# Two neighbouring rows of the down weights on one partition, and a strided transpose to match, in a streaming encoder step

## Chip, cores and metric

The kernel runs on one core of one Trainium2 chip. The metric is the device time of one execution in microseconds (us); the median of 3 runs is 1451.0 us, between 1450.89 and 1451.71.

## What is computed

One inference step of a two-layer encoder for 384 frames of width 1024 (256 of a new stream, 16 of each of 8 running ones). Each layer has a mixer (a causal convolution group and a pooling group between the projections w_in and w_out) and then a channel mixer: dense SwiGLU in layer 0, the two best of eight SwiGLU experts in layer 1. The channel mixers are what this case is about:

```python
D_MODEL, D_FF, EXPERT_FF, N_EXPERTS, TOP_K = 1024, 2816, 2816, 8, 2

def swiglu(h, wg, wu, wd):
    return jnp.einsum('blf,fd->bld',
                      jax.nn.silu(jnp.einsum('bld,df->blf', h, wg)) * jnp.einsum('bld,df->blf', h, wu), wd)

def moe_swiglu(h, router_w, router_b, wg, wu, wd):
    ...
    for e in range(N_EXPERTS):
        out = out + gates[..., e:e + 1].astype(h.dtype) * swiglu(h, wg[e], wu[e], wd[e])
    return out
```

All data are float32.

## The kernel before

Every engine's program is written out by hand, with semaphores between the engines; no scheduler moves anything.

**Precision.** A float32 product is made of three products of halves: a weight tile `raw` is copied to `w_hi` in a rounded form (ScalarE, `make_hi`, line 260), `w_lo = raw - w_hi` is made by VectorE (`make_lo`, line 264), and `product` (lines 284 to 286) issues three matmuls, hi by hi, hi by lo, lo by hi.

**Weight tiles.** The 2816 hidden columns of a channel mixer are cut into `NF` = 11 pieces of 256. A piece has three tiles of 1 MB (128 partitions of 2048 floats): gate and up (1024 input rows by 256 columns, in memory 1 KB runs), and down (256 hidden rows by 1024 columns, rows of 4 KB). `raw`, `w_hi` and `w_lo` have six slots each: two pieces. SyncE issues the loads in the order in which they are used (`sp_tile`, line 350, calls `load`, line 252): a slot's next load waits until `make_lo` has read the slot (`lo_ready`). ScalarE's `make_hi` waits for the landing, and, in `act_ffn_tile` (line 525), for the matmuls that read the slot of `w_hi` before.

**One unit**, that is one piece of 256 hidden columns for one block of 128 tokens. The dense mixer has 11 pieces for 3 blocks of tokens, 33 units; the expert mixer has one gathered block an expert, 8 x 11 = 88 units. 121 in all. On TensorE (`pe_unit`, line 1140) unit l makes

- `unit_gu` (line 1098): 24 matmuls of 512 columns, gate and up side by side into one PSUM bank, tokens on the partitions,
- `unit_turn` (line 1117) of the unit before: two transposes of `act_b` (128 tokens by 256 hidden columns), so that hidden rows lie on the partitions,
- `unit_down` (line 1123) of the unit two before: 12 matmuls of 512 columns with `ft_hi` and `ft_lo` (the transposed activations, halved by `act_ft`, line 538, and `ft_low`, line 835) as the loaded operand and the down tile as the streamed one.

In a transpose and in a matmul alike the first operand after the output is loaded into the array (LDWEIGHTS, the engine PEld of the profile) and the second streams through it. In `unit_turn` the loaded one is `act_b`, the streamed one the identity:

```python
for i in range(2):
    ins = pe.transpose(ps[:, f.bank(l), i * P:(i + 1) * P], act_b[:, i * P:(i + 1) * P], ident[:, :])
```

Transpose i gives hidden rows 128 i to 128 i + 127, so row p of half i on partition p; the source of a down tile (`ffn_src`, line 328) puts rows p and p + 128 on partition p, one after the other, which is what `unit_down` streams for i = 0 and i = 1.

Between experts TensorE gathers the next expert's tokens (`gather`, line 1167, 48 small matmuls) and scatters the last one's results (`scatter`, line 1178).

Of the kernel before, what the change touches and what calls it, by code (L numbers as in the profile page):

```python
# [25 lines left out]
P = 128  # L26
# [12 lines left out]
FT = 256  # L39
# [50 lines left out]
def build(nc, a):  # L90
    ctx = ExitStack()
    with ctx:
# [3 lines left out]
        def place(name, floats, dt=F32, offset=None, parts=P):  # L96
            o = at["next"] if offset is None else offset
            t = nc.alloc_sbuf_tensor_at(name, [parts, floats], dt, offset=base + o)
            if offset is None:
                at["next"] = (o + floats * 4 + 31) // 32 * 32  # L100
            at[name] = o
            return t
# [14 lines left out]
        ident = place("ident", P)  # L117
# [25 lines left out]
        act_b = place("act_b", FT, offset=s0 + 5120)  # L143
# [29 lines left out]
        ps = ctx.enter_context(nc.psum_tensor("ps", [P, 8, 512], F32))  # L173
# [17 lines left out]
        def y_sb(c):  # L191
            return ext[:, c * WIN:(c + 1) * WIN]

        def y_sq(c):
            o = NCB * CEXT + c * WIN
            return ext[:, o:o + WIN]
# [85 lines left out]
        def product(pe, out, lh, ll, rh, rl, start, stop):  # L282

            pe.matmul(out, lh, rh, start=start, stop=False)  # L284
            pe.matmul(out, lh, rl, start=False, stop=False)  # L285
            return pe.matmul(out, ll, rh, start=False, stop=stop)  # L286
# [41 lines left out]
        def ffn_src(w, kind, e, c):  # L328

            m = w[kind][0]  # L330
            if len(m.shape) == 3:
                if kind == "d":
                    rows = m.rearrange("e (c k p) n -> (e c) p k n", p=P, k=2)
                    return rows[bass.ds(e * NF + c, 1)].rearrange("o p k n -> (o p) k n")
                m = m[bass.ds(e, 1)].rearrange("o a b -> (o a) b")
            if kind == "d":
                return m[bass.ds(c * FT, FT), :].rearrange("(k p) n -> p k n", p=P)
            return m.rearrange("(k p) n -> p k n", p=P)[:, :, bass.ds(c * FT, FT)]


# [9 lines left out]
        def sp_tile(sp, f, w, e, kind, c, c_expr):  # L350
            load(sp, f.slot(kind, c), f.uses(kind, c), ffn_src(w, kind, e, c_expr), 2 if kind == "d" else KD)
# [730 lines left out]
        def _(pe):  # L1082
# [10 lines left out]
            def blk(ap, i, width=TOK):  # L1093
                return ap[:, i * width:(i + 1) * width]
# [22 lines left out]
            def unit_turn(f, l):  # L1117
                pe.wait_ge(S["act_done"], f.count(l + 1))
                for i in range(2):
                    ins = pe.transpose(ps[:, f.bank(l), i * P:(i + 1) * P], act_b[:, i * P:(i + 1) * P], ident[:, :])  # L1120
                ins.then_inc(S["turned"], 1)

            def unit_down(f, l, shift):
# [16 lines left out]
            def pe_unit(f, l, shift, item):  # L1140
                static = isinstance(f.step, int)
                true = l + shift if item is not None and static else None
                prev = item is not None and item.prev is not None
                if true == 0:
                    pe.wait_ge(S["xT_lo"], 2 * item.n + 2)
                unit_gu(f, l)
                if true == 0:
                    turn_one_hot(item)
                if prev and true in SCATTER:
                    scatter(item.prev[0], 1 - item.parity, SCATTER[true])  # L1150
                if l > 0 or prev:
                    unit_turn(f, l - 1)
                if l > 1 or prev:
                    if true == 2 and prev:
                        pe.wait_ge(S["ye_lo_ready"], 2 * item.prev[0] + 2)
                    unit_down(f, l - 2, shift)
                if true == 9 and item.nxt is not None:
                    gather(item.nxt[0])
# [30 lines left out]
            for l in range(LAYERS):  # L1189
                pe_hT(2 * l, range(NTB))  # L1190
                if l == 0:
# [5 lines left out]
                    for i in range(LAYERS):  # L1197
                        n = TAPS * NCB
                        ins = pe.transpose(ps[:, 6, C_CW + i * n:C_CW + (i + 1) * n],
                                           prm_rows[0:n, (1 + i) * P:(2 + i) * P], ident[0:n, 0:n])  # L1200
# [8 lines left out]
                for j in range(12):  # L1209
                    s, m = divmod(j, 2)  # L1210
# [9 lines left out]
                    for k in range(KD):  # L1220
                        o = s * TILE + k * 256 + m * P
                        ins = product(pe, ps[:, WIN_BANK[j], 0:TOK], w_hi[:, o:o + P], w_lo[:, o:o + P],
                                      blk(a_hi, k), blk(a_lo, k), k == 0, k == KD - 1)
                    ins.then_inc(S["blk_done"], 1)
                    if j == 1:
# [6 lines left out]
                        for c in range(NCB):  # L1232
                            for g in range(3):
                                rows = hist[0:120, g * CH + c * P:g * CH + (c + 1) * P]
                                ins = pe.transpose(ps[:, 2 + c, g * 120:(g + 1) * 120], rows, ident[0:120, 0:120])
# [38 lines left out]
                def w_out(s, tb):  # L1274
                    for i in range(2):
                        e = 2 * WOUT_TILES[s] + i
                        for dh in range(2):
                            o, m = e * TOK + tb * P, WOUT_SLOT[s] * TILE + i * D + dh * 512
                            ins = product(pe, ps[:, 2 * tb + dh, :], a_hi[:, o:o + P], a_lo[:, o:o + P],
                                          w_hi[:, m:m + 512], w_lo[:, m:m + 512], s == 0 and i == 0, s == 3 and i == 1)  # L1280
                    return ins
# [4 lines left out]
                for c in range(NCB):  # L1286
                    pe.wait_ge(S["y_ready"], 4 * l + c + 1)
                    ins = pe.matmul(ps[:, 6, 0:TOK], mean_w[:, :], y_sb(c), start=c == 0, stop=c == NCB - 1)  # L1288
# [3 lines left out]
                for tb in range(NTB):  # L1292
                    ins = w_out(0, tb)
                ins.then_inc(S["wout_used"], 1)
                pe.wait_ge(S["sq_done"], 4 * (l + 1))
                for c in range(NCB):
                    ins = pe.matmul(ps[:, 7, 0:TOK], mean_w[:, :], y_sq(c), start=c == 0, stop=c == NCB - 1)
                ins.then_inc(S["var_done"], 1)
                pe.wait_ge(lo_ready[WOUT_SLOT[1]], GEN_WOUT[l][1] + 1)
                for tb in range(NTB):  # L1300
                    ins = w_out(1, tb)
# [12 lines left out]
                if l == 0:  # L1314
                    pe_hT(1, [1])

                    def dense_unit(f, l, shift):
                        if l < NTB and shift == 0 and isinstance(f.step, int):
                            if l == 1:
                                pe_hT(1, [2])  # L1320
                            if l == 2:
                                pe.wait_ge(S["x_added"], 6)
                            pe.wait_ge(S["hT_lo"], ht_count(1, l, 1))
                        pe_unit(f, l, shift, None)
                    units_loop(pe, dense, dense_unit)
                    unit_turn(dense, DENSE_UNITS - 1)
                    unit_down(dense, DENSE_UNITS - 2, 0)
                    unit_down(dense, DENSE_UNITS - 1, 0)
# [5 lines left out]
            for k in range(KD):  # L1334
                ins = product(pe, ps[0:NE, 2, 0:TOK], rw_hi[:, k * NE:(k + 1) * NE], rw_lo[:, k * NE:(k + 1) * NE],
                              blk(a_hi, k), blk(a_lo, k), k == 0, k == KD - 1)
            ins.then_inc(S["logits_done"], 1)
            pe.wait_ge(S["lgt_ready"], 1)
            for tb in range(NTB):
                ins = pe.transpose(ps[:, 4, tb * NE:(tb + 1) * NE], lgt[0:NE, tb * P:(tb + 1) * P], ident[0:NE, 0:NE])  # L1340
# [6 lines left out]
            for tb in range(NTB):  # L1347
                ins = pe.matmul(ps[:, 3, (tb + 1) * NE:(NTB + 1) * NE], mean_w[:, :], mask[:, 0:(NTB - tb) * NE],
                                start=False, stop=tb == NTB - 1)
# [6 lines left out]
            def finish(f, item):  # L1356
                unit_turn(f, NF - 1)
                unit_down(f, NF - 2, 0)
                unit_down(f, NF - 1, 0)
                pe.wait_ge(S["ye_lo_ready"], 2 * item.n + 2)  # L1360
                scatter(item.n, item.parity, range(6))
# [145 lines left out]
```

## Time and profile before

| | |
|---|---|
| median of 3 runs | 1451.0 us |
| profiled execution, span from first to last instruction (no other time of this execution is listed) | 1453.4 us |
| TensorE matmul busy (PE) | 1380.2 us, 95% |
| weight loads into the array (PEld) | 1152.1 us, 79% |
| VectorE (DVE) | 1041.2 us, 72% |
| ScalarE (ACT) | 792.8 us, 55% |
| moved by DMA | 343.13 MB, mean 236 GB/s |

The span of the profiled execution is 2.4 us above the median. The dense mixer runs from about 165 us to 440 us of the span, the expert mixer from about 620 us to 1440 us. A matmul's end is modelled in the profile, so where matmuls follow each other the distance between two starts says what one costs, not its duration. "Landing" of a DMA is counted from its issue.

### The profile page before, as it was taken

To read this page: it belongs to the slowest core of one execution; us is meant where nothing else is said; L and a number is where in the kernel's file an instruction comes from. 1 tells how busy PE (TensorE), PEld (TensorE's weight loads), DVE (VectorE), ACT (ScalarE), POOL (GpSimd) and SP (SyncE) were. 2 spreads that over 40 slices of the span, in tenths; PEclk is the share of its full clock that TensorE was granted. 3 is DMA by queue.
4 is the path that set the end of the run, shared out by engine and by line. 5 is a ranking of instruction groups with operands and counts; after the bars stand their busy time and mean duration, and the time that the engine had idled before them with its cause. 6 is when DMAs were issued, how large, how long until landed. Compare 5 with 4: busy or idle time off the path is not lost.

```text
span 1453.4 us, 17788 instructions
## 1 busy us (share of the span) xinstructions
PE 1380.2 (95%) x6492; PEld 1152.1 (79%) x6493; DVE 1041.2 (72%) x1196; ACT 792.8 (55%) x892; POOL 69.2 (5%) x120
## 2 busy tenths in 40 slices
PE   5999899999998989689999999999999999999994
PEld 5986788888887977578888888888888888888883
DVE  4795633333327795568799798898887997997984
ACT  5554322232215553367677677665776766766752
POOL 1050100000000231000000000000000000000000
PEclk9999999999998999799999999999999999999997
DMA  9114433433143114379999999999999999999971
GB/s 314 67 53 159 159 116 119 141 117 117 51 150 98 47 52 124 111 261 366 332 344 358 326 348 363 312 342 367 328 347 321 348 353 324 354 355 323 346 261 70
DMA packets 252825, 343.13 MB, mean 236 GB/s; under 512 B 6252, under 2 KB 222724, under 8 KB 252758
## 3 DMA queue, kind: packets, MB, share of 16 engines
q1 hardware_dynamic: 249542, 335.78, 68.6%
q0 software_dynamic: 1424, 4.31, 1.0%
q10 hardware_dynamic: 1792, 2.18, 0.4%
q8 instruction: 39, 0.64, 0.2%
q14 instruction: 28, 0.23, 0.0%
HBM read 339.01 MB, written 3.23 MB: 235 GB/s over the span
## 4 chain that ended last, share of the span: by engine, by line
PE 85%; DVE 10%; ACT 2%; issue 1%; DMA 1%; POOL 0%; SPq 0%; DVEq 0%; POOLq 0%; ACTq 0%
PE ps L284 26%; PE ps L286 25%; PE ps L285 25%; DVE ps L818 5%; PE ps L1173 3%; PE ps L1120 2%; DVE w_lo L264 1%; DMA raw<-in_w_in 1%; PE ps L1184 1%; PE ps L1186 1%; PE ps L1288 1%; DVE ext L778 1%; ACT ext L504 1%; DVE x L900 1%; DVE a_lo L785 1%
## 5 line engine op out<-in xcount | busy, mean ns | idle before, releaser
L264 DVE TENSOR_TENSOR w_lo<-raw,w_hi 128x2048 fp32r<-128x2048 f32 x317 | 717.2, 2288 | 126.9 <-ACT w_hi L260 126.7
L260 ACT ACTIVATE w_hi<-raw 128x2048 fp32r<-128x2048 f32 x317 | 596.3, 1916 | 4.9 <-DMA raw<-in_w_in 4.1
L284 PE MATMUL ps<-w_hi,a_hi 128*128 128x512 f32 x1064 | 419.8, 395 | 8.2 <-DVE ft_lo L838 5.5
L286 PE MATMUL ps<-w_hi,a_lo 128*128 128x512 f32 x1064 | 415.7, 391 | 0.0
L285 PE MATMUL ps<-w_lo,a_hi 128*128 128x512 f32 x1064 | 415.7, 391 | 0.0
L543 ACT ACTIVATE ft_hi<-ps 128x256 fp32r<-128x256 f32 x121 | 46.5, 385 | 390.5 <-PE ps L1120 390.5
L284 PEld LDWEIGHTS ps<-w_hi,a_hi 128*128 128x128 f32 x1064 | 200.6, 189 | 54.3 <-issue 8.4
L286 PEld LDWEIGHTS ps<-w_hi,a_lo 128*128 128x128 f32 x1064 | 200.5, 188 | 42.0
L285 PEld LDWEIGHTS ps<-w_lo,a_hi 128*128 128x128 f32 x1064 | 200.7, 189 | 41.3 <-issue 0.6
L284 PE MATMUL ps<-w_hi,ft_hi 128*128 128x512 f32 x484 | 200.9, 415 | 0.0
L286 PE MATMUL ps<-w_hi,ft_lo 128*128 128x512 f32 x484 | 191.5, 396 | 0.0
L285 PE MATMUL ps<-w_lo,ft_hi 128*128 128x512 f32 x484 | 191.1, 395 | 0.0
L838 DVE TENSOR_TENSOR ft_lo<-ps,ft_hi 128x256 fp32r<-128x256 f32 x121 | 51.0, 421 | 146.7 <-ACT ft_hi L543 146.7
L818 DVE SCALAR_TENSOR_TENSOR ps<-ext,prm,ps 128x256 f32<-128x256 f32 (+1 forms) x360 | 109.9, 397 | 0.0
L286 PEld LDWEIGHTS ps<-w_hi,ft_lo 128*128 128x128 f32 x484 | 91.3, 189 | 20.7
L285 PEld LDWEIGHTS ps<-w_lo,ft_hi 128*128 128x128 f32 x484 | 91.9, 190 | 16.4
L284 PEld LDWEIGHTS ps<-w_hi,ft_hi 128*128 128x128 f32 x484 | 92.1, 190 | 16.0
L284 PE MATMUL ps<-a_hi,w_hi 128*128 128x384 f32 x192 | 66.3, 345 | 6.6 <-DVE a_lo L785 6.6
L1377 POOL TENSOR_TENSOR stat<-stat,mhalf 128x1 f32<-128x1 f32 x15 | 12.2, 817 | 1187.0 <-DVE stat L771 1187.0
L285 PE MATMUL ps<-a_lo,w_hi 128*128 128x384 f32 x192 | 65.4, 341 | 0.0
L286 PE MATMUL ps<-a_hi,w_lo 128*128 128x384 f32 x192 | 65.3, 340 | 0.0
L832 DVE TENSOR_TENSOR act_b<-ps,silu 128x256 f32<-128x256 f32 x121 | 50.5, 417 | 8.8 <-ACT silu L536 8.8
(151 smaller groups left out, 957.7 us busy)
## 6 DMA issues: line engine op xcount, KB each, us to landing
raw<-in_moe_w_gate SPq DMA_DIRECT2D x88, 1024.0 KB, 7.5
raw<-in_moe_w_up SPq DMA_DIRECT2D x88, 1024.0 KB, 8.3
raw<-in_moe_w_down SPq DMA_DIRECT2D x88, 1024.0 KB, 7.5
raw<-in_w_in SPq DMA_DIRECT2D x12, 1024.0 KB, 12.0
raw<-in_dense_w_gate SPq DMA_DIRECT2D x11, 1024.0 KB, 5.4
raw<-in_dense_w_up SPq DMA_DIRECT2D x11, 1024.0 KB, 5.4
raw<-in_dense_w_down SPq DMA_DIRECT2D x11, 1024.0 KB, 5.0
raw<-in_w_out SPq DMA_DIRECT2D x8, 1024.0 KB, 5.1
```

Of the source, the lines that this page charges most:

```text
L260: act.activation(slot(w_hi, s), slot(raw, s), ACT.Copy).then_inc(hi_ready[s], 1)
L264: dve.tensor_tensor(slot(w_lo, s), slot(raw, s), slot(w_hi, s).bitcast(F32), ALU.subtract)\
L284: pe.matmul(out, lh, rh, start=start, stop=False)
L285: pe.matmul(out, lh, rl, start=False, stop=False)
L286: return pe.matmul(out, ll, rh, start=False, stop=stop)
L504: act.activation(ext[:, tb * D:(tb + 1) * D], x[:, tb * D:(tb + 1) * D], ACT.Square, accum_out=stat[:, tb:tb + 1]).then_inc(S["ssq_done"], 1)
L543: act.activation(ft_hi[:, b * FT:(b + 1) * FT], ps[:, f.bank(l), 0:FT], ACT.Copy)\
L818: ins = dve.scalar_tensor_tensor(out=o, in0=src, scalar=w, in1=o, op0=ALU.mult, op1=ALU.add)
L832: dve.tensor_tensor(act_b[:, :], ps[:, f.bank(l), FT:2 * FT], silu[:, :], ALU.mult)\
L838: dve.tensor_tensor(ft_lo[:, b * FT:(b + 1) * FT], ps[:, f.bank(l), 0:FT], ft_hi[:, b * FT:(b + 1) * FT].bitcast(F32), ALU.subtract)\
L1120: ins = pe.transpose(ps[:, f.bank(l), i * P:(i + 1) * P], act_b[:, i * P:(i + 1) * P], ident[:, :])
L1173: ins = pe.matmul(ps[:, 2 + i, (k % 4) * P:(k % 4 + 1) * P], h[:, tb * D + k * P:tb * D + (k + 1) * P], onehot[:, tb * P:(tb + 1) * P], st ...
```

## The change

The down tile's source has rows 2p and 2p + 1 of the 256 on partition p, which lie next to each other in memory: 8 KB in one run where there were two runs of 4 KB. The two transposes take the even and the odd columns of `act_b`, so that half i of the transposed activations has hidden row 2p + i on partition p.

```diff
                 if kind == "d":
-                    rows = m.rearrange("e (c k p) n -> (e c) p k n", p=P, k=2)
+                    rows = m.rearrange("e (c p k) n -> (e c) p k n", p=P, k=2)
                     return rows[bass.ds(e * NF + c, 1)].rearrange("o p k n -> (o p) k n")
                 m = m[bass.ds(e, 1)].rearrange("o a b -> (o a) b")
             if kind == "d":
-                return m[bass.ds(c * FT, FT), :].rearrange("(k p) n -> p k n", p=P)
+                return m[bass.ds(c * FT, FT), :].rearrange("(p k) n -> p k n", k=2)
...
                 for i in range(2):
-                    ins = pe.transpose(ps[:, f.bank(l), i * P:(i + 1) * P], act_b[:, i * P:(i + 1) * P], ident[:, :])
+                    ins = pe.transpose(ps[:, f.bank(l), i * P:(i + 1) * P], act_b[:, i::2], ident[:, :])
                 ins.then_inc(S["turned"], 1)
```

No instruction is added, taken away or moved on any engine, and no wait changes. In SyncE's program the 99 issues of a down tile have the shape 128 x 2048 floats where they had 128 x 2 x 1024; each stays at its place between the gate and up tiles.

## Rows read from the trace of the kernel before

**Rows 1.** The page: TensorE, its clock, and DMA in 40 slices.
```profile
PE   5999899999998989689999999999999999999994
PEclk9999999999998999799999999999999999999997
DMA  9114433433143114379999999999999999999971
```

**Rows 2.** The page: the chain that ended last, by engine and by line.
```profile
PE 85%; DVE 10%; ACT 2%; issue 1%; DMA 1%; POOL 0%; SPq 0%; DVEq 0%; POOLq 0%; ACTq 0%
PE ps L284 26%; PE ps L286 25%; PE ps L285 25%; DVE ps L818 5%; PE ps L1173 3%; PE ps L1120 2%; DVE w_lo L264 1%; DMA raw<-in_w_in 1%; PE ps L1184 1%; PE ps L1186 1%; PE ps L1288 1%; DVE ext L778 1%; ACT ext L504 1%; DVE x L900 1%; DVE a_lo L785 1%
```

**Rows 3.** Windows, 640 to 1390 us: busy time by engine, clock, DMA share, GB/s.
```profile
core 0: us, PE busy (x) PEld busy (x) DVE busy (x) ACT busy (x) POOL busy (x), PEclk, DMA share, GB/s
640.00:1390.00 750.00, 750.00 (x3548) 621.77 (x3547) 649.47 (x496) 514.32 (x445) 0.00 (x0) 1.00 1.01 344
```

**Rows 4.** Waits of ScalarE, 640 to 1390 us: total us, times, longest us.
```profile
ACT ft_hi L543 <- PE ps L1120: 182.4, 75, 3.4
ACT a_hi L574 <- PE ps L286: 52.8, 7, 7.5
ACT ye_hi L582 <- PE ps L286: 2.6, 7, 0.4
```

**Rows 5.** Waits of the whole run: the one that a weight tile's DMA ended.
```profile
ACT w_hi L260 <- DMA raw<-in_w_in: 4.1, 3, 2.1
```

**Rows 6.** Timeline around one unit's two transposes: start us, length us, engine, instruction.
```profile
1391.93 0.39 PE L286 MATMUL ps<-w_hi,a_lo 128*128 128x512 f32 x1
1391.93 0.37 PEld L1120 LDWEIGHTS ps<-ident,act_b 128*128 128x128 f32 x2
1392.16 0.38 PE L1120 MATMUL ps<-ident,act_b 128*128 128x128 f32 x2
1392.27 0.19 PEld L284 LDWEIGHTS ps<-w_hi,ft_hi 128*128 128x128 f32 x1
1392.30 0.48 PE L284 MATMUL ps<-w_hi,ft_hi 128*128 128x512 f32 x1
1392.61 0.39 PE L285 MATMUL ps<-w_lo,ft_hi 128*128 128x512 f32 x1
```

**Rows 7.** Line 1120 in the whole run: duration in ns, min/median/max.
```profile
L1120 PEld LDWEIGHTS ps<-ident,act_b x242: 137/138/143, 169.9 to 1423.8; 128*128 128x128 f32 x121
L1120 PE MATMUL ps<-ident,act_b x242: 271/273/328, 170.0 to 1423.9; 128*128 128x128 f32 x121
```

**Rows 8.** DMA issues, 165 to 380 us: count, KB each, median us to landing.
```profile
raw<-in_dense_w_down SPq DMA_DIRECT2D x9, 1024.0 KB, 5.0
raw<-in_dense_w_gate SPq DMA_DIRECT2D x8, 1024.0 KB, 5.3
raw<-in_dense_w_up SPq DMA_DIRECT2D x8, 1024.0 KB, 5.4
```

**Rows 9.** The one DMA issued between 996.0 and 996.5 us.
```profile
raw<-in_moe_w_up SPq DMA_DIRECT2D x1, 1024.0 KB, 11.2
```

**Rows 10.** Timeline: that issue, and ScalarE's copies of this gate and up tile.
```profile
996.10 0.37 SPq L256 DMA_DIRECT2D raw<-in_moe_w_up  x1
...
1006.96 3.71 ACT L260 ACTIVATE w_hi<-raw 128x2048 fp32r<-128x2048 f32 x2
```

**Rows 11.** The page: DMA packets by size.
```profile
DMA packets 252825, 343.13 MB, mean 236 GB/s; under 512 B 6252, under 2 KB 222724, under 8 KB 252758
```

**Rows 12.** Last down tile, 1414.5 to 1425 us: DMA view, then timeline.
```profile
raw<-in_moe_w_down SPq DMA_DIRECT2D x1, 1024.0 KB, 4.9
1421.58 1.91 ACT L260 ACTIVATE w_hi<-raw 128x2048 fp32r<-128x2048 f32 x1 [0.32 <-PE ps L286]
```

**Rows 13.** The tile `raw`, same stretch: its last DMA's issue.
```profile
L256 SPq DMA_DIRECT2D raw<-in_moe_w_down x1: 367/367/367, 1414.9 to 1414.9; - x1
```

**Rows 14.** Timeline: three down matmuls, then three gate-and-up matmuls.
```profile
1385.80 0.39 PE L286 MATMUL ps<-w_hi,ft_lo 128*128 128x512 f32 x1
1386.03 0.39 PE L284 MATMUL ps<-w_hi,ft_hi 128*128 128x512 f32 x1
1386.26 0.39 PE L285 MATMUL ps<-w_lo,ft_hi 128*128 128x512 f32 x1
...
1388.76 0.39 PE L284 MATMUL ps<-w_hi,a_hi 128*128 128x512 f32 x1
1388.98 0.39 PE L285 MATMUL ps<-w_lo,a_hi 128*128 128x512 f32 x1
1389.21 0.39 PE L286 MATMUL ps<-w_hi,a_lo 128*128 128x512 f32 x1
```

## The prediction

> **What bounds the kernel now.** I read the slices first. Over the last 60% of the span, the expert mixer, TensorE and the DMA engines both show nines [rows 1], so the slices cannot say which of the two sets the pace; the question of this case is which one does, because the change works on both. The chain of waits answers for the whole: 85% of the span is TensorE, 76% the three matmul lines of `product` [rows 2]. The window from 640 to 1390 us answers for the expert mixer: TensorE is busy for 750.00 of 750 us at the full clock (granted 1.00, the 2.4 GHz level), while the DMA share is 1.01 at 344 GB/s [rows 3]. What decides is who waits. ScalarE, the first to touch a landed tile, waits there only for TensorE (182.4 and 52.8 and 2.6 us) and never for a DMA [rows 4]; the only weight tiles in the whole run's list of waits are three of w_in, 4.1 us [rows 5], which the change leaves alone. So the DMA engines are full but not late, and TensorE sets the end.
>
> How close to late? The tightest tile I found is an up tile issued at 996.10 us, which landed 11.2 us later, at 1007.3 [rows 9, 10]. ScalarE copies a gate and an up tile from 1006.96 to 1010.67, and the second copy starts about 1.86 us in, at 1008.8. The margin is 1.5 us. It is smallest there because inside an expert TensorE eats tiles faster than they come, and it is won back while TensorE gathers the next expert's tokens. So each expert has 1.5 us to spare over its 11 pieces.
>
> **The change part by part.**
>
> *The down loads.* 99 tiles are read in 128 runs of 8 KB instead of 256 of 4 KB; bytes, place in the queue and issue count stay. The trace has no 8 KB run of weights, so the price is bounded by neighbours. In the dense mixer, where loads mostly have the queue to themselves, a tile in 1024 runs of 1 KB lands in 5.3 to 5.4 us and one in 256 runs of 4 KB in 5.0 us [rows 8]: 768 runs fewer saved 0.35 us. By the same slope 128 runs fewer save 0.35 x 128 / 768 = 0.06 us a tile. That is my estimate, 0.06 us x 99 = 6 us of DMA time. One end of the range is a gain as large as the last step, 0.35 us a tile; the other is a tile that becomes as slow as one of 1 KB runs, 0.35 us more. On the path the gain is worth nothing at either size: it only lengthens a margin that nobody uses. The cover is TensorE's work, 750 of 750 us; in the dense mixer, with 9 tiles landed in 5.0 us while a piece lasts three units, the cover is larger still. A loss counts only past the margin: 1.5 us / 11 tiles = 0.14 us a tile.
>
> *The end of the program.* The last down tile has no work of an expert behind it. It is issued at 1414.9 us [rows 13] and lands 4.9 us later, at 1419.8; ScalarE's copy starts at 1421.58, held by a matmul [rows 12]. Here too the load is 1.8 us early. Gain: 0.
>
> *The transposes.* 242 of them load `act_b` with a step of two floats instead of one. This is the part that lies on the path: nothing hides TensorE. Before, the first load runs beside the last gate-and-up matmul: it starts at 1391.93, takes 0.138 us [rows 7], and the transpose follows at 1392.16, so 0.09 us of room is left. The second load starts with the first transpose, and the next weights start at 1392.27 [rows 6]: 0.11 us a transpose, set by the load. The trace has no strided load into the array, so again two ends. Lower end: no change, 0 (a gain is excluded: the same 128 columns are loaded, from twice as wide a stretch). Upper end: a load takes twice as long. The first then sticks out of its cover by 0.138 - 0.09 = 0.05 us, the second costs 0.11 more: 0.16 us a unit, x 121 units = 19 us. (Were neither hidden at all, 2 x 0.138 x 121 = 33 us.) I take 0, by the nearest row: a streaming matmul reads 512 floats, 2048 bytes of each partition, in 0.225 us [rows 14], which is 9.1 bytes per ns, and a strided load would sweep 128 x 8 = 1024 bytes in 0.11 us, 9.3 bytes per ns. An operand is already read at that pace in this kernel, though through the streaming side.
>
> The Trainium skill, SBUF — State Buffer, section "Specifications (TRN2)", bears on this and cuts both ways. It says that the memory is read in lines of 16 bytes, that two hits a line are needed for full speed, and that each crossing to a new line pays. Every second float gives exactly two hits a line, so by the first half the sum stays 0; by the second half there are twice as many crossings as with a step of one, and the sum would go towards the upper end. No row here shows a strided load into the array.
>
> *VectorE, ScalarE, SyncE.* `act_b` is written as before, and `ft_hi`, `ft_lo` and the down slots are read by the same addresses. 0.
>
> Sum: 0 + 0 + 0 against the profiled 1453.4 us. That span is 2.4 us (0.17%) above the median of the runs, 1451.0 us, and since no term is a share of it, the forecast is the median: **1451.0 us**.
>
> **Rivals.**
>
> *A, the stride costs TensorE time (slower).* Place: `unit_turn`, 121 times, on the path. It decides as soon as a unit's two transposes take 0.024 us longer (121 x 0.024 = 2.9 us, 0.2%, about what a measurement of this kernel can tell from no change). Price with a halved load rate: +19 us, 1470 us. For it: the load sets the pace there, 0.11 us each [rows 6]. Against: the pace of the streaming reads.
>
> *B, 8 KB runs are slower, and DMA becomes the bound (slower).* The DMA engines have no time left (share 1.01, rows 3). If a down tile costs 0.35 us more, an expert's 11 tiles cost 3.85 us, of which the margin takes 1.5; 2.35 us x 8 experts = 19 us, 1470 us. ScalarE would be the first to wait. Against: fewer runs went with a shorter landing in rows 8.
>
> *C, TensorE gains (faster).* Down matmuls start 0.23 us apart, gate-and-up ones 0.225 us [rows 14]. If the 0.005 us had to do with how the down tiles come in, 12 x 121 x 0.005 = 7.3 us could go, 1444 us. Against: the tile lies in the same slot in the same layout when TensorE reads it, and landed long before.
>
> *D, the change does not do what it says.* The hardware could cut an 8 KB run into the 4 KB pieces of before. The time would be that of the forecast; only the packet count would tell.
>
> **How the numbers follow.** No change, the forecast, D included: 0.76. A: 0.10. B: 0.07. C: 0.07. Hence faster 0.07, same 0.76, slower 0.17. The forecast case alone spans 1448.1 to 1453.9. To reach 8 in 10 I keep it whole and add the small prices of A and B, up to 0.066 us a unit or 8 us, for some 0.04 of chance: 1448.0 to 1459.0. The full prices of A and B near 1470 and C near 1444 are the 2 in 10 left out.
>
> **What the profile after would show.** Right: the weight load of line 1120 stays at 138 ns and the next weights still start 0.11 us after the second transpose; TensorE busy for the whole of a window in the expert mixer; ScalarE waits for no down tile; dense down tiles land in about 4.9 us. If the runs are really 8 KB, 99 x 128 = 12,672 packets fewer than 252,825 [rows 11], 240,153, and 25,344 fewer under 8 KB; an unchanged count is D. Wrong by A: the load of line 1120 nearer 0.28 us, and the pair's stretch longer. Wrong by B: waits of ScalarE on a moe tile and gaps on TensorE between 640 and 1390 us. Wrong by C: down matmuls closer than 0.23 us.

## The result, and the profile after

The changed kernel takes 1455.85 us (median), the kernel before, run beside it, 1451.82 us: a ratio of 1.0031, 95% interval 1.0021 to 1.0041. It is slower by 4 us; the interval reaches from 3.0 to 6.0 us. One of the nine executions of the changed kernel took 1759.1 us at a mean granted clock of 0.74 and is left out of the ratio. The prediction said no change. The time lies in its range, but on the side to which it gave 0.17.

The profiled execution of the changed kernel took 1458.8 us, its span is 1457.0 us. The page of after, beside [rows 1, 2, 11]: TensorE, its clock and DMA in 40 slices, the DMA packets, the chain by engine.

```profile
PE   5999899999998989689999999999999999999994
PEclk9999999999998999799999999999999999999997
DMA  9114433433142114279999999999999999999971
DMA packets 240153, 343.13 MB, mean 236 GB/s; under 512 B 6252, under 2 KB 222724, under 8 KB 227414
PE 85%; DVE 10%; ACT 2%; issue 1%; DMA 1%; POOL 0%; SPq 0%; DVEq 0%; POOLq 0%; ACTq 0%
```

The packet count is the predicted one to the last packet, 240,153 in all, and under 8 KB there are 25,344 fewer than before (227,414): the runs are really 8 KB, and rival D is out. The bound has not moved: 85% of the chain is TensorE, as before.

DMA issues of after, 165 to 380 us, beside [rows 8]: count, KB each, median us to landing.

```profile
raw<-in_dense_w_down SPq DMA_DIRECT2D x9, 1024.0 KB, 4.7
raw<-in_dense_w_gate SPq DMA_DIRECT2D x8, 1024.0 KB, 5.4
raw<-in_dense_w_up SPq DMA_DIRECT2D x8, 1024.0 KB, 5.2
```

A down tile lands 0.3 us earlier, at the far end of the bounds of the prediction. Nobody waited for it before and nobody does now. Waits of ScalarE in after, 640 to 1390 us, beside [rows 4]:

```profile
ACT ft_hi L543 <- PE ps L1120: 185.0, 75, 4.8
ACT a_hi L574 <- PE ps L286: 52.8, 7, 7.6
ACT ye_hi L582 <- PE ps L286: 2.6, 7, 0.4
```

No DMA in that list: rival B is out. The same stretch as a window, beside [rows 3], and a second, short one at the start of the expert mixer:

```profile
core 0: us, PE busy (x) PEld busy (x) DVE busy (x) ACT busy (x) POOL busy (x), PEclk, DMA share, GB/s
640.00:1390.00 750.00, 750.00 (x3542) 625.56 (x3542) 646.63 (x495) 510.89 (x443) 0.00 (x0) 1.00 1.00 342
635.00:640.00 5.00, 4.08 (x11) 3.24 (x12) 5.00 (x5) 3.68 (x3) 0.00 (x0) 0.66 1.06 350
```

TensorE has no gap in either kernel, but it issues 3542 matmuls in 750 us where it issued 3548, and its loads are busy 3.8 us longer. So it does the same work a little more slowly. The line that the change touches is 1120. Its durations in after, beside [rows 7]:

```profile
L1120 PEld LDWEIGHTS ps<-ident,act_b x242: 194/197/216, 169.8 to 1427.4; 128*128 128x128 f32 x121
L1120 PE MATMUL ps<-ident,act_b x242: 272/282/385, 169.9 to 1427.5; 128*128 128x128 f32 x121
```

The strided load takes 197 ns instead of 138. What that does to the path is read from the starts. The timeline of after around one unit's transposes, beside [rows 6]:

```profile
1395.46 0.40 PE L286 MATMUL ps<-w_hi,a_lo 128*128 128x512 f32 x1
1395.46 0.43 PEld L1120 LDWEIGHTS ps<-ident,act_b 128*128 128x128 f32 x2
1395.69 0.39 PE L1120 MATMUL ps<-ident,act_b 128*128 128x128 f32 x2
1395.80 0.20 PEld L284 LDWEIGHTS ps<-w_hi,ft_hi 128*128 128x128 f32 x1
1395.84 0.48 PE L284 MATMUL ps<-w_hi,ft_hi 128*128 128x512 f32 x1
1396.15 0.39 PE L285 MATMUL ps<-w_lo,ft_hi 128*128 128x512 f32 x1
```

The next weights still start 0.11 us after the first transpose, so the pair of transposes is as dense as before. The loss lies at its two edges. Over the 78 units in the middle of the expert mixer the medians of the starts, in ns, are:

| from, to | before | after |
|---|---|---|
| last gate-and-up matmul, first transpose | 231 | 235 |
| first transpose, second transpose | 108 | 108 |
| second transpose, first down matmul | 28 | 38 |
| first down matmul, second down matmul | 316 | 315 |

The medians add up to 13 ns a unit. By the means of the four together, which some longer units raise, a unit is 14.3 ns longer (0.6722 to 0.6865 us). Times 121 units that is 1.7 us: 0.47 us in the 33 dense units and 1.26 us in the 88 of the experts. As a cross-check, one expert took 101.45 us from scatter to scatter and now takes 101.61: 0.16 x 8 = 1.3 us. This leaves some 2 us of the 4 open, and the experiments had to find both: which part of the change it is, and what the rest is. In this pair of profiles one more difference is seen at once: between 635 and 640 us the granted clock is 0.66 in after, where it was 1.00 before.

### The profile page after: what moved, and what is told of

It reads as the page before. It is cut to its first block, busy times and chain, and to the rows that moved or that the text cites. A ratio compares the mean times of both kernels' runs of the same rounds, so it can differ in the third digit from the quotient of the medians.

```text
span 1457.0 us, 17788 instructions
## 1 busy us (share of the span) xinstructions
PE 1384.0 (95%) x6492; PEld 1160.6 (80%) x6493; DVE 1040.9 (71%) x1196; ACT 792.9 (54%) x892; POOL 69.2 (5%) x120
## 2 busy tenths in 40 slices
DMA packets 240153, 343.13 MB, mean 236 GB/s; under 512 B 6252, under 2 KB 222724, under 8 KB 227414
## 4 chain that ended last, share of the span: by engine, by line
PE 85%; DVE 10%; ACT 2%; issue 1%; DMA 1%; POOL 0%; SPq 0%; DVEq 0%; POOLq 0%; ACTq 0%
PE ps L284 26%; PE ps L286 26%; PE ps L285 25%; DVE ps L818 5%; PE ps L1173 3%; PE ps L1120 2%; DVE w_lo L264 1%; DMA raw<-in_w_in 1%; PE ps L1184 1%; PE ps L1186 1%; DVE ext L778 1%; PE ps L1288 1%; ACT ext L504 1%; DVE x L900 1%; DVE a_lo L785 1%
```

## The experiments

In all runs the kernel before ran beside the others on the same chip; its medians there were between 1451.4 and 1452.7 us.

**One part of the change at a time.** The first kernel has the 8 KB runs with the old transposes, the second the strided transposes with the old runs. In both, hidden rows and down rows are not paired as in the reference, while instructions and sizes are those of the change. The edit of the second:

```diff
-                    ins = pe.transpose(ps[:, f.bank(l), i * P:(i + 1) * P], act_b[:, i * P:(i + 1) * P], ident[:, :])
+                    ins = pe.transpose(ps[:, f.bank(l), i * P:(i + 1) * P], act_b[:, i::2], ident[:, :])
```

> The 8 KB runs alone; the transposes take adjacent columns as before, so hidden rows and down rows are paired otherwise than in the reference. Theory S (the strided load of act_b costs TensorE time, the runs nothing): within 0.1% of the kernel before, line 1120 loads in 138 ns, an expert's period 101.45 us. Rival R (the 8 KB runs themselves cost the 4 us): 1455 to 1456 us, 0.3% slower, with 138 ns loads.

> The strided transposes alone, down tiles in 4 KB runs as before (pairing again not the reference's). Theory S: line 1120 loads in 197 ns, an expert's period 101.6 us, and the time as slow as the whole change, 1453.5 to 1456 us; 121 units x 0.014 us = 1.7 us is the steady part, anything above it shows as stretches of the 1.2 GHz clock level. Rival R: the time of the kernel before, 1451.8 us.

> The whole change again on the same chip as the others. Both theories: 1454 to 1459 us. Theory S adds that the executions fall into groups about 3 to 4 us apart, and that the slower group has the lower mean granted clock; if the clock does not go with the time, the part above 1.7 us has another cause.

| kernel | median, us | ratio to before | load of the transposes, ns | one expert, us |
|---|---|---|---|---|
| 8 KB runs alone | 1452.55 | 1.0002 (0.9993 to 1.0011) | 139 | 101.45 |
| stride alone | 1455.11 | 1.0022 (1.0013 to 1.0031) | 197 | 101.62 |
| the change again | 1456.35 | 1.0029 (1.0018 to 1.0039) | 197 | 101.61 |

Line 1120 with the stride alone:

```profile
L1120 PEld LDWEIGHTS ps<-ident,act_b x242: 194/197/216, 170.3 to 1424.0; 128*128 128x128 f32 x121
```

The longer runs cost nothing and bring nothing that these intervals could show, as predicted. The strided transposes are the whole difference, within the intervals. The second half of the last expectation did not come: the time does not go with the mean granted clock of an execution. The change took 1454.3 us at 0.981 and 1459.1 us at 0.976, but 1455.0 us at 0.977 and 1456.4 us at 0.978. By that expectation's own sign this speaks against the clock. But the mean does not show where the clock was low (of the profiles below, two with the same stretches of low clock in the experts and behind them have means of 0.981 and 0.977), so the question is taken up again there, place by place.

**The stride moved to VectorE.** Here VectorE parts the even from the odd columns when it writes `act_b`, and the transposes load contiguous columns:

```diff
-                dve.tensor_tensor(act_b[:, :], ps[:, f.bank(l), FT:2 * FT], silu[:, :], ALU.mult)\
+                dve.tensor_tensor(act_b[:, :].rearrange("p (k n) -> p n k", k=2),
+                                  ps[:, f.bank(l), FT:2 * FT].rearrange("p (n k) -> p n k", k=2),
+                                  silu[:, :].rearrange("p (n k) -> p n k", k=2), ALU.mult)\
```

> 8 KB runs as in the change, but VectorE writes even columns to the first half of act_b and odd ones to the second, so the transposes load adjacent columns; the pairing is that of the change. Theory S: within 0.1% of the kernel before, loads of 138 ns; VectorE's product at line 832 may take longer than 415 ns, which nothing waits for as long as it stays under about 1 us. Rival R: 0.3% slower, 1455 to 1456 us.

It took 1455.89 us, 1.0024 (1.0014 to 1.0034): no better than the change. The load is back at 139 ns, but the product takes 630 ns. Its row in this kernel:

```profile
L832 DVE TENSOR_TENSOR act_b<-ps,silu x121: 601/630/651, 168.8 to 1423.1; 128x256 f32<-128x256 f32 x121
```

and in the kernel before:

```profile
L832 DVE TENSOR_TENSOR act_b<-ps,silu x121: 411/417/425, 169.4 to 1423.2; 128x256 f32<-128x256 f32 x121
```

One expert takes 101.71 us, 0.26 more than before. The loss is not at the transposes. Some 0.16 us of it is at the first gate-and-up matmul of the next unit, which starts 245 ns after the last down matmul instead of 230 (means of 78 units; the medians are 227 in both). In each expert two units make this: one waits 375 ns where it waited 256, one 266 to 281 where it did not stand out. In all of these the matmul starts 146 ns after VectorE has finished `ft_lo`, as it did in the unit of 256 ns: the product, 0.21 us longer, makes `ft_lo` later. VectorE is busy for 72% of the span and was taken to have room for this; it has none in the two units where TensorE waits for it.

**A longer step.** Transposes that read every third float of an `act_b` widened to 384 floats:

```diff
-                    ins = pe.transpose(ps[:, f.bank(l), i * P:(i + 1) * P], act_b[:, i * P:(i + 1) * P], ident[:, :])
+                    ins = pe.transpose(ps[:, f.bank(l), i * P:(i + 1) * P], act_b[:, i::3], ident[:, :])
```

> The kernel before, but the transposes load every third float of a buffer of 384 (the last third of it zeros), so they turn other columns than the reference asks for. If the strided load's price follows the stretch of memory that it sweeps, the load of line 1120 takes about 250 ns (138, then 197 at a step of two, again about 60 ns more) and a unit's price on TensorE is at least twice the 0.014 us of step two: 1455 to 1460 us. If every other float was a fixed price of not being adjacent, 197 ns and the time of the stride alone, 1455 us.

```profile
L1121 PEld LDWEIGHTS ps<-ident,act_b x242: 189/197/212, 169.4 to 1428.1; 128*128 128x128 f32 x121
```

The load takes 197 ns again: between these two steps it pays for columns that are not adjacent, not for the distance swept. The kernel took 1457.59 us, 1.0034 (1.0022 to 1.0046), and an expert 101.84 us: 0.010 us a unit, 0.11 us of the 0.39 that an expert lost, is at its transposes; the rest is spread over the other matmuls, about 1 ns on many of their starts. Why, these runs do not tell.

**The stride in one mixer only.** In the experts alone (88 units, the edit below) or, with the condition turned round, in the dense mixer alone (33 units):

```diff
-                    ins = pe.transpose(ps[:, f.bank(l), i * P:(i + 1) * P], act_b[:, i * P:(i + 1) * P], ident[:, :])
+                    ins = pe.transpose(ps[:, f.bank(l), i * P:(i + 1) * P], act_b[:, i::2] if f.nb == 1 else act_b[:, i * P:(i + 1) * P], ident[:, :])
```

> Strided transposes in the 88 expert units alone (pairing not the reference's there). By the steady part alone 88 x 0.0143 = 1.26 us: 1453.5 us. If the part above the steady 1.7 us comes behind the expert mixer, in the program's end, it is all here: 1455 us; if it comes between the dense and the expert mixer, 1453.5 us.

> Strided transposes in the 33 dense units alone (pairing not the reference's there). By the steady part alone 33 x 0.0143 = 0.47 us: 1452.7 us. If the rest comes in the pauses between the two mixers, up to 2 us more, 1454 to 1455 us; if it comes at the end, 1452.7 us.

The experts alone: 1454.12 us, 1.0008 (0.9999 to 1.0017). The dense mixer alone: 1453.62 us, 1.0003 (0.9994 to 1.0012). The means lie 1.5 and 0.4 us above that of the kernel before; their sum, 1.9 us, is what the units show, and less than the whole change costs. So neither mixer alone brings a rest that these runs could show: the experts, 1.3 us longer in their units, cost 1.5.

**Is the rest the clock?** After a pause of TensorE the profiles often show a stretch at the 1.2 GHz level. Three runs asked whether that is the rest. The first adds unneeded transposes worth as much as the strided loads, the other two fill TensorE's two pauses (ahead of the second expert unit and ahead of the last transposes) with unneeded matmuls, in the kernel before and in the change:

```diff
+                for n in extra:
+                    pe.transpose(ps[0:n, f.bank(l), 0:P], act_b[:, 0:n], ident[:, :])
```

```diff
+            def busy(n):
+                for i in range(n):
+                    pe.matmul(ps[:, 2, :], a_hi[:, 0:P], a_hi[:, 0:512], start=True, stop=True)
...
+                if true == 1 and isinstance(item.n, int) and item.n == 0:
+                    busy(13)
...
+                busy(10)
```

> The kernel before with adjacent columns and 4 KB runs, and with as much TensorE time added as the stride costs by the trace, in another way: 4 more transposes in the dense mixer (4 x 0.108 = 0.43 us) and one of 128 and one of 64 columns an expert (0.16 x 8 = 1.3 us), 1.7 us in all. Theory S1 (the stride costs 1.7 us, and any 1.7 us at these places would be followed by 1.5 to 2 us more at the lower clock): 1455 to 1456 us. Theory S2 (what is above 1.7 us belongs to the strided load itself): 1454.0 us.

> The kernel before, with TensorE kept at work at two places where it otherwise pauses: 13 extra matmuls (into a bank that nobody reads) ahead of the second unit of the expert mixer, 10 ahead of the last pair of transposes. They stand in pauses and should move nothing else; what the added instructions themselves do to the time is not known, so this run is the base for the next one, not a gain. Both theories: within 4 us of the kernel before. Theory S (the clock drops after these pauses): in the profile no stretch at the 1.2 GHz level right behind the first units of the expert mixer, nor at the last down matmuls.

> The same fillers in the changed kernel. Theory S: the strided loads cost 1.7 us in steady work (0.0143 us x 121) and the remaining 1.5 to 2 us of the difference is clock drops after the two pauses, which the fillers prevent: 1.7 us above the run with fillers in the kernel before. Rival R (the remainder is in the units themselves, or in pauses elsewhere): 3.2 to 4.1 us above it, as without fillers. Between 2.2 and 2.8 us neither is told apart.

All three were inconclusive. The transposes: 1460.48 us, 1.0055 (1.0042 to 1.0069); they cost 0.27 us an expert and not the intended 0.16, and one expert's half period was 52.23 us, once, where the others took 49.14. The fillers: 1456.07 us in the kernel before and 1458.88 us in the change. Their two profiles show no stretch at the 1.2 GHz level at either place, as expected, but both show the same kind of pause in one expert (53.70 and 53.39 us for 48.87 and 48.95). The difference of the two, 2.8 us, is neither of the values expected, and the change with fillers scatters from 1455.7 to 1463.8 us. Added instructions disturb this program by more than what was to be measured.

The profiles show something beside that pause. In the kernel before, the DMA queue q8, for instructions, carries 39 packets, none of them between 1005 and 1220 us; in each of these three kernels it carries 48, nine of them in that window, and three of the nine lie between 1017 and 1025 us, around the pause. From 1015 to 1030 us, the first of the fillers:

```profile
q8 instruction: 3, 0.05, 1.3%
```

and TensorE's only wait from 960 to 1080 us, for nothing that the profile shows:

```profile
PE ps L284 <- issue: 2.9, 1, 2.9
```

So the pause may be a wait for instructions; no run here tested that.

**The same lengthening without a strided load.** The next edit adds no instruction. The second transpose of some pieces streams the identity with a step of two and writes its columns with the same step; all loads are contiguous. The first kernel is shown, the second lists the pieces (0, 2, 4, 6, 8, 10):

```diff
+                    out, one = ps[:, f.bank(l), i * P:(i + 1) * P], ident[:, :]
+                    if i == 1 and l // f.nb in (1, 4, 8):
+                        out = out.rearrange("p (n j) -> p j n", j=2)
+                        one = one.rearrange("p (n j) -> p j n", j=2)
+                    ins = pe.transpose(out, act_b[:, i * P:(i + 1) * P], one)
```

> The kernel before, all weights loaded contiguously; in 3 of 11 pieces (33 of the 121 units) the second transpose streams the identity with a step of two and writes its 128 columns with the same step. The streaming run showed that a streamed step of two takes twice as long: 128 columns, some 0.054 us more a unit, if none of it is hidden, 33 x 0.054 = 1.8 us, spread over the dense and the expert mixer as the change's own 1.7 us is. Theory S (the change costs 1.7 us in the units, and the longer stages shift the later pauses so that the clock falls to 1.2 GHz in more of them): 3 to 4 us above the kernel before, like the change, with no strided load. Rival R (the rest belongs to strided loads themselves): what the units show, 1.8 us or less, and no more.

> The same in 6 of 11 pieces (66 units): by the units 66 x 0.054 = 3.6 us if none is hidden. Rival R: twice the one with 3 pieces. Theory S: not in proportion; the difference between the run and the price read in its units goes up and down with the shift, between 0 and 3 us.

> The change again, on the chip of the two runs with a shift, as their yardstick: 3.2 to 4.1 us above the kernel before, expert period 101.61 us.

The load of the transposes in the first kernel:

```profile
L1124 PEld LDWEIGHTS ps<-ident,act_b x242: 137/139/143, 169.7 to 1422.7; 128*128 128x128 f32 x121
```

| kernel, by the pieces asked for | median, us (before: 1451.38) | ratio to before | one expert, us | dense mixer, us |
|---|---|---|---|---|
| 3 pieces | 1454.81 | 1.0028 (1.0016 to 1.0039) | 101.58 | 264.65 |
| 6 pieces | 1454.82 | 1.0025 (1.0014 to 1.0036) | 101.59 | 264.72 |
| the change again | 1454.72 | 1.0026 (1.0014 to 1.0038) | 101.62 | 264.69 |

The mixers did become longer, though not where it was expected: the pair of transposes and the first down matmul keep their starts to the ns, and of the matmuls after them some follow the one ahead 4 to 10 ns later, others earlier. Nor are the units those that the expectations count. The loop over the pieces repeats one body, and `l // f.nb` is the piece's number in that body: the traces show the later starts in pieces 1, 4, 6 and 8 of each expert in the first kernel and in pieces 0, 2, 4, 6 and 8 in the second. With the dense mixer, counted from the program, these are 43 and 59 of the 121 units and not 33 and 66.

For the first kernel the sum is 0.13 us an expert, 1.0 us for eight, and 0.3 us in the dense mixer (264.35 us in a profile of the kernel before with the same clock there), 1.3 us in all. For the second, with 1.4 times as many units, it is 0.14 us an expert and 0.4 us in the dense mixer, 1.5 us in all: nearly a repeat of the first, and no test of twice the length. Both cost 3.4 us. So a kernel without any strided load, whose units are longer by 1.3 us, is slower by as much as the change, whose units are longer by 1.7. Rival R of these runs, that a rest comes with strided loads alone, falls.

**Where the clock stands in the profiles.** The last three runs are the kernel before again, for its profile.

> The kernel before once more, for its profile: after TensorE's pause ahead of the last two transposes (some 2.2 us, for act_b) the clock stays at 2.4 GHz while the last 24 down matmuls run, and the stretch from the last pair of transposes to the end is 28.4 us, not 29.7 as in all seven profiles of kernels with longer expert units. If it shows 29.7 us as often as not, the clock at the end does not tell the two kernels apart and the remainder of the difference stays open.

> As the run ahead of it: 28.4 us at the end, full clock in the last 24 down matmuls.

> As the two runs ahead of it: 28.4 us at the end, full clock in the last 24 down matmuls.

Two of three missed: they show the slower end. Windows of the first of these repeats of the kernel before, at the start of the experts and at the last down matmuls:

```profile
core 0: us, PE busy (x) PEld busy (x) DVE busy (x) ACT busy (x) POOL busy (x), PEclk, DMA share, GB/s
630.00:635.00 5.00, 1.79 (x9) 1.23 (x8) 4.84 (x4) 5.00 (x6) 0.00 (x0) 1.00 0.27 75
...
1424.00:1428.00 4.00, 4.00 (x14) 3.20 (x13) 2.23 (x2) 0.39 (x1) 0.00 (x0) 0.65 0.00 0
```

The third repeat:

```profile
630.00:635.00 5.00, 3.06 (x9) 2.45 (x10) 5.00 (x5) 4.69 (x4) 0.00 (x0) 0.77 0.94 312
...
1424.00:1428.00 4.00, 4.00 (x19) 3.13 (x17) 0.72 (x2) 0.00 (x0) 0.00 (x0) 1.00 0.00 0
```

The change, as run beside the lengthened kernels:

```profile
630.00:635.00 5.00, 3.45 (x10) 2.76 (x11) 5.00 (x5) 4.31 (x4) 0.00 (x0) 0.73 1.01 331
...
1424.00:1428.00 4.00, 4.00 (x12) 3.09 (x11) 1.48 (x2) 0.00 (x0) 0.00 (x0) 0.57 0.00 0
```

Its timeline at the last transposes:

```profile
1423.00 0.50 PE L1120 MATMUL ps<-ident,act_b 128*128 128x128 f32 x2 [2.16 <-DVE act_b L832]
...
1424.04 0.51 PE L284 MATMUL ps<-w_hi,ft_hi 128*128 128x512 f32 x1
1424.35 0.63 PE L285 MATMUL ps<-w_lo,ft_hi 128*128 128x512 f32 x1
1424.78 0.63 PE L286 MATMUL ps<-w_hi,ft_lo 128*128 128x512 f32 x1
```

TensorE pauses for 2.16 us, starts again at the full clock, and a microsecond later its matmuls stand 0.43 us apart instead of 0.23. In the kernel before, exactly one of the two places has such a stretch; in the change both can. The profiles of the kernels that differ by the runs or by a stride in the transposes alone, from the starts of the transposes:

| kernels | 1.2 GHz stretch, first expert units | at the last down matmuls | experts, us | last transposes to the end, us | together |
|---|---|---|---|---|---|
| before: three profiles | no | yes | 792.3 to 792.4 | 29.7 to 29.8 | 822.0 to 822.1 |
| before (one), 8 KB runs alone, stride in dense alone | yes | no | 793.8 to 794.0 | 28.3 to 28.6 | 822.2 to 822.4 |
| the change (two), stride alone, 3 pieces | yes | yes | 794.9 to 795.2 | 29.7 | 824.5 to 824.9 |
| the change (one), stride in experts alone, 6 pieces | no | yes | 793.3 to 793.6 | 29.4 to 29.9 | 823.0 to 823.5 |

Like has to be compared with like. Where the first place has no stretch, the longer experts cost 0.9 to 1.5 us, about what their units show, and the end is the same. Where it has one, they cost 2.1 to 2.6 us: the units, and 1.1 to 1.3 us at the end, where the last down matmuls now run into a stretch that the old length escaped. This second part is the clock's share, in four of seven profiles, 0.7 us on average.

The two groups of longer profiles can't be set against each other, though their means (824.7 and 823.2 us) differ by 1.5 us. With a stretch at the first expert units the way to them from the last transposes of the dense mixer was shorter in most profiles (193.3 to 193.8 us, in two 196.1, against 195.4 to 195.7 without one). Counted from those transposes to the end both groups take the same on average, 1018.8 and 1018.7 us: what is lost at the first expert units was saved ahead of them.

With the units' 1.7 us this makes 2.4 us on average and 2.9 us where the stretch at the end falls, against medians 3.3 to 4.1 us apart. The interval of the first comparison begins at 3.0 us, that of the last at 2.0 us (0.0014 x 1451.4). How often that stretch falls in executions that leave no profile is not known; the last microsecond or so of the difference has no place that these runs show.

Nor does a longer expert mixer always bring it. Two profiles with still longer experts, which the first of the last three expectations overlooks, run their last down matmuls at the full clock and end like the kernel before: the product written apart (794.3 us of experts, 28.1 us at the end, no stretch at either place) and the step of three (797.0 and 28.4 us, a stretch at the first). With the stride in the experts alone there is a stretch at the end, as there is before, and the cost is about that of the units. What is shown is that a rest can come without a strided load, and that at one place it is the clock; that the clock is all of it is not.

**Streaming with a step of two.** Last, a version that keeps both the 8 KB runs and contiguous transposes: the gate and up weights are streamed with a step of two floats, so that `act_b` comes out already parted.

```diff
-                    return w[:, s * TILE:(s + 2) * TILE].rearrange("p (g k n) -> p g k n", g=2, k=KD)[:, :, k, :]
+                    return w[:, s * TILE:(s + 2) * TILE].rearrange("p (g k n i) -> p g k i n", g=2, k=KD, i=2)[:, :, k]
```

> 8 KB runs, but act_b comes out of the gate and up matmuls already parted into even and odd columns: the streamed weights are read with a step of two floats (24 matmuls of 512 columns a unit), and the transposes load contiguous columns again. If a step of two costs the streaming side nothing (the prediction's comparison of paces would then be right for that side): expert period 101.45 us, load of the transposes 138 ns, 1452 to 1453 us. If it costs the streaming side even 1% (2.3 ns a matmul): 24 x 121 x 0.0023 = 6.6 us more. If the streaming halves its pace: 24 x 121 x 0.225 = 650 us more.

It took 2106.16 us, 1.4502 (1.4483 to 1.4521). The timeline of this kernel in an expert:

```profile
999.74 0.63 PE L285 MATMUL ps<-w_lo,a_hi 128*128 128x512 f32 x1
1000.19 0.63 PE L286 MATMUL ps<-w_hi,a_lo 128*128 128x512 f32 x1
1000.64 0.63 PE L284 MATMUL ps<-w_hi,a_hi 128*128 128x512 f32 x1
```

The matmuls stand 0.45 us apart, at the full clock. (2106.16 - 1452.67) / (24 x 121) = 0.225 us more each: half the pace. No version tried beats the kernel before.

## Why the prediction was wrong

**The step that failed** is the value taken for the transposes: "I take 0, by the nearest row". The part was named rightly (the only one on the path) and its bounds held the truth, 0 and 19 us, with 1.7 us measured in the units. But the load did become longer, from 138 to 197 ns, and the lower end was not the one to take. Rival A named the place and the direction, but not the price: it was to decide from 0.024 us a unit, the units showed 0.014, and only with the rest, which it did not foresee, was the kernel slower by more than 0.2%.

**The comparison behind it** set the sweep of a strided load against the pace of the streamed operand, 9.1 bytes per ns. The streaming run shows what that pace means: with a step of two, 512 columns sweep 4096 bytes in 0.45 us, 9.1 bytes per ns again. On the streaming side the step is paid in full. On the loading side the price did not grow with the sweep, since a step of two and one of three take the same 197 ns. A row on one side of TensorE priced nothing on the other. The comparison also took 0.11 us, the distance of the two transposes, for the time of a load; the load's own 138 ns [rows 7] would have given 7.4 bytes per ns, and the strided load measured 1024 bytes in 197 ns, 5.2.

**The mechanism of the upper end** was wrong as well. The first load was to stick out of its cover of 0.09 us when it grew past that: it grew by 0.059, stays inside, and still costs 4 ns. The second was to set a slower pace between the transposes, as if the 0.11 us between them were "set by the load": it doesn't (0.108 us, unchanged, with a load of 138 ns and with one of 197). The next weights start with the second transpose [rows 6], 0.11 us after the first and not after the second, as the prediction reads it. The 10 ns come one step later, between the second transpose and the first down matmul, where the load of the first down weights takes 0.20 us instead of 0.19; that this load is the reason is not shown.

**What the sum left out** is the rest, some 2 us. A forecast that adds up durations takes each pause's aftermath as fixed. Here a stretch of low clock at the last down matmuls, in four of seven profiles, makes 1.1 to 1.3 us of it; the cause of the remainder stays open. That 1.3 us more in the units, made without any strided load, moved the time by 3.4 us shows that a rest of this size needs no strided load.

**What held.** The down loads: 0 on the path, and 1.0002 for the 8 KB runs alone. The gain in landing was 0.3 us, at the bound and not the 0.06 that I took, and worth nothing. The end of the program: the last down tile was early, landed at 1423.6 us and copied from 1425.2. Rivals B, C and D: no wait for a tile, no gain, and the predicted packet count.

The Trainium skill, SBUF — State Buffer, section "Specifications (TRN2)", was cited for both ends: two hits a 16-byte line for full speed, and a price for each crossing to a new line. The runs agree with the second half for the direction of the load (138 to 197 ns), though a step of three, which crosses to a new line more often still, took 197 ns too. They disagree with the first half on the streaming side: with every second float, two hits a line, the pace was half.

## What to carry to other kernels

Put a stride where nothing on the path reads through it: the weight loads partly hid it (two of 59 ns more each, 14 ns on the path), the streamed operand of 512 columns took twice as long, VectorE's product 1.5 times. When an operand's price has no row, take one short run of that operand rather than a row of another port. And where a bound engine pauses, a microsecond more in its work can come back as three (1.3 us came back as 3.4 here): before you explain a difference of 0.2%, compare the granted clock right behind each pause in several profiles, and set side by side only those that agree at the pauses ahead. Where a loop repeats one body, check in the trace which units an edit has reached.

## What the runs showed of the hardware that was not expected

- A load of 128 x 128 floats into the array takes 138 ns contiguous, 197 ns with a step of two and 197 ns with a step of three.
- A matmul that streams 512 floats a partition with a step of two takes 0.45 us, twice 0.225. For a transpose that streams 128 columns the same step does not delay the next matmul (28 ns after it in both cases); some of those behind it follow 4 to 10 ns later.
- A DMA tile of 1 MB in 128 runs of 8 KB lands in 4.7 us, in 256 runs of 4 KB in 5.0 us [rows 8], medians of nine in the dense mixer.
- After TensorE's pauses a stretch at 1.2 GHz came or did not come in different executions of the same kernel, and the pause alone does not decide it: ahead of the last transposes it lasted 2.16 us both in the change, where the clock fell, and with the 8 KB runs alone, where it stayed full.
- Unneeded matmuls in two pauses made one expert 5 us longer at a place where nothing was added, and brought nine more packets of instructions in the middle of the expert mixer.
